# Rows on two queues, context turned later, and second projections in turns with a norm

## The reference

```python
def rms_norm(x, g):
    return x * lax.rsqrt(jnp.mean(x * x, axis=-1, keepdims=True) + EPS) * g
# first block, layer 0
hn = rms_norm(x, g_pre[0])
proj = hn @ ssm_w_in          # z, xBC and dt: dt is 32 columns wide
# between the blocks: the final norm of the first, and the first norm of the second
h = rms_norm(h, g_final)
hx = modulate(rms_norm_2(h, norm1), shift, scale)
# second block: keys, values, low-rank gate inputs (lr, 32 columns) of tokens and context
hx @ w_in; hc @ w_in[:, :CTX_COLS]
# MLP: squared ReLU, 1024 -> 4096 -> 1024
h = h + gate * (jnp.square(jax.nn.relu(modulate(rms_norm_2(h, norm2)) @ w_mlp1)) @ w_mlp2)
```

## Time and profile before

| | |
|---|---|
| median of three runs | 1840.89 us (1839.2 to 1844.04) |
| the profiled execution | 1845.2 us, its span 1843.4 us |
| PE busy | 1756.7 us, 95% |
| DVE busy | 1004.4 us, 54% |
| ACT busy | 798.3 us, 43% |
| POOL busy | 713.5 us, 39% |
| mean granted clock of PE | 0.981 |

### The profile page before, as it was taken

The page is one execution under the profiler, slowest core; times in us unless marked ns, Lnnn a source line. Parts: engine busy times, 40 slices in busy tenths (PEclk is TensorE's granted clock), DMA queues, the critical chain, the costliest instruction groups (busy, mean ns, idle before and its releaser), DMA issues.

```text
span 1843.4 us, 24950 instructions
## 1 busy us (share of the span) xinstructions
PE 1756.7 (95%) x8893; PEld 1401.0 (76%) x8893; DVE 1004.4 (54%) x1545; ACT 798.3 (43%) x1359; POOL 713.5 (39%) x795
## 2 busy tenths in 40 slices
PE   7999999988999889899999999999999989999998
PEld 5778777766776557678878788888878768888887
DVE  5788786677346773356649737656733341212122
ACT  4345463555456663345542235554432342323131
POOL 3644544434352105221113422223234645555553
PEclk9999999999999999999999999999999989999999
DMA  6342423121222002111028711121123323333332
GB/s 199 96 132 74 134 74 87 58 69 54 75 80 64 24 12 61 53 45 29 24 77 271 223 46 35 35 58 46 46 80 93 101 69 93 102 92 101 92 97 98
DMA packets 238794, 152.04 MB, mean 82 GB/s; under 512 B 7997, under 2 KB 223046, under 8 KB 238694
## 3 DMA queue, kind: packets, MB, share of 16 engines
q1 hardware_dynamic: 225894, 125.54, 23.6%
q10 hardware_dynamic: 12800, 25.17, 4.0%
HBM read 148.59 MB, written 2.10 MB: 82 GB/s over the span
## 4 chain that ended last, share of the span: by engine, by line
PE 65%; issue 12%; POOL 8%; DVE 8%; ACT 6%; DMA 1%; SPq 1%; POOLq 0%; DVEq 0%; ACTq 0%
PE ps L650 16%; PE ps L654 16%; PE ps L651 16%; POOL wl L600 8%; PE ps L2093 2%; PE ps L2075 1%; PE ps L1574 1%; PE ps L1606 1%; PE ps L2082 1%; PE ps L2555 1%; DMA ada_late<-w_ada 1%; DVE mod_late L2407 1%; DVE queries L1843 1%; PE ps L2076 1%; DVE pairs L2785 1%
## 5 line engine op out<-in xcount | busy, mean ns | idle before, releaser
L600 POOL TENSOR_TENSOR wl<-raw,wh 128x256 fp32r<-128x256 f32 (+1 forms) x775 | 690.1, 920 | 1070.1 <-ACT wh L613 1070.1
L650 PE MATMUL ps<-ah,wh 128*128 128x512 f32 (+1 forms) x1144 | 467.0, 408 | 16.5 <-DVE al L762 9.8
L654 PE MATMUL ps<-ah,wl 128*128 128x512 f32 (+1 forms) x1144 | 450.9, 394 | 0.1
L651 PE MATMUL ps<-al,wh 128*128 128x512 f32 (+1 forms) x1144 | 450.3, 394 | 0.0
L613 ACT ACTIVATE wh<-raw 128x1024 fp32r<-128x1024 f32 (+1 forms) x220 | 230.9, 1049 | 315.9 <-PE ps L654 302.7
L650 PEld LDWEIGHTS ps<-ah,wh 128*128 128x128 f32 (+1 forms) x1144 | 216.3, 189 | 78.2 <-issue 19.6
L654 PEld LDWEIGHTS ps<-ah,wl 128*128 128x128 f32 (+1 forms) x1144 | 216.1, 189 | 50.6 <-POOL wl L600 1.4
L651 PEld LDWEIGHTS ps<-al,wh 128*128 128x128 f32 (+1 forms) x1144 | 216.7, 189 | 45.0 <-issue 1.4
L650 PE MATMUL ps<-bh,wh 128*128 128x512 f32 (+1 forms) x588 | 233.7, 397 | 8.9 <-DVE bl L1427 3.3
L654 PE MATMUL ps<-bh,wl 128*128 128x512 f32 (+1 forms) x588 | 230.5, 392 | 0.9 <-POOL wl L600 0.8
L651 PE MATMUL ps<-bl,wh 128*128 128x512 f32 (+1 forms) x588 | 230.3, 392 | 0.0
(11 more groups left out here) (422 smaller groups left out, 2698.7 us busy)
## 6 DMA issues: line engine op xcount, KB each, us to landing
raw<-w_mlp SPq DMA_DIRECT2D x64, 512.0 KB, 3.8
raw<-w_in SPq DMA_DIRECT2D x52, 512.0 KB, 3.7
raw<-ssm_w_in SPq DMA_DIRECT2D x40, 512.0 KB, 3.8
ada_late<-w_ada ACTq DMA_DIRECT2D x16, 1024.0 KB, 6.8
ada_raw<-w_ada ACTq DMA_DIRECT2D x16, 512.0 KB, 3.7
raw<-ssm_w_out SPq DMA_DIRECT2D x16, 512.0 KB, 3.4
raw<-mla_w_in SPq DMA_DIRECT2D x11, 512.0 KB, 3.7
raw<-mla_w_out SPq DMA_DIRECT2D x8, 512.0 KB, 3.4
```

The lines of the kernel that those rows point to most:

```text
L600: nc.gpsimd.tensor_tensor(wl[:, s, part], raw[:, s, part], wh[:, s, part].bitcast(F32), ALU.subtract).then_inc(lo_ready, LOW_PIECES * (par ...
L650: nc.tensor.matmul(dst, w_hi[k], x_hi[k], start=k == 0, stop=False)
L651: nc.tensor.matmul(dst, w_hi[k], x_lo[k], start=False, stop=False)
L654: ins = nc.tensor.matmul(dst, w_lo[k], x_hi[k], start=False, stop=k == n - 1)
```

## The change

Four edits:

1. The 18 transfers of vector rows are divided: SP issues every other one (`row_sources[0::2]`), ACT the others at its very start.
2. Context's transposes move from ahead of "dt" to behind unit 1 of "ssm_first" (`turn_ctx`); ACT's four copies move behind its copy of unit 1, and DVE's wait for them moves to before the memset of `conv_in`.
3. In the second block the two norm sums come ahead of the context value tiles, "final" gets bank 4 for its own (with a wait before the second key unit, which writes that bank). `project_v` goes over chunks outside and tiles inside and waits for low pieces one by one. "lr" and the token tiles of value unit 0 run in turns, two chunks of "lr" and one of values.
4. The first MLP block is written out of the loop, and its units 0 and 1 run chunk by chunk in turns behind the norm.

```diff
+        def load_rows(eng, sources):
+            for name, col in sources:
+                v = as_rows(ins[name])
+                eng.dma_start(vrows[col % P:col % P + v.shape[0], col // P, :], v).then_inc(rows_in, 16)
...
@@ pe_start
-            pe.wait_ge(sem("ctx_in"), 16)
-            pe.wait_ge(sem("x_copied"), DC)
-            for c in range(DC):
-                for t in range(CTX // P):
-                    ins_ = nc.tensor.transpose(bank(CTX_BANKS[c // 2])[:, c % 2 * CTX + t * P:c % 2 * CTX + (t + 1) * P],
-                                               ctx_tok[:, t, c * P:(c + 1) * P], ident[:])
-                if c % 2:
-                    ins_.then_inc(sem("ctx_turned"), 1)
@@ pe_mamba
+            def turn_ctx():
...
             for n in range(1, 10):
                 projection("ssm_first", 0, n)
-                if n == 3:
+                if n == 1:
+                    turn_ctx()
+                elif n == 3:
                     turn_dt()
@@ act_start
             count_ahead(act, "act")
+            load_rows(act, row_sources[1::2])
             nc.scalar.preload_act_table_set(LN_EXP)
@@ act_mamba
-            take_ctx(0)
             split_ahead(act, "dt", 0, 0)
...
-            for c in range(2, DC, 2):
+            take_conv("ssm_first", 0, 0, 1)
+            for c in range(0, DC, 2):
                 take_ctx(c)
-            take_conv("ssm_first", 0, 0, 1)
@@ dve_start, dve_mamba
-            dve.wait_ge(sem("ctx_turned"), DC // 2)
...
+            dve.wait_ge(sem("ctx_turned"), DC // 2)
             st(nc.vector.memset(conv_in[:, :, 0:PAD], 0.0))
@@ act_between
-        GAINED_BANK = 7
+        GAINED_BANK, FINAL_BANK = 7, 4
...
-            norm_act(act, "final", None, D, dst=norm_sq[:, 1])
+            norm_act(act, "final", None, D, b=FINAL_BANK, dst=norm_sq[:, 1])
@@ pe_gqa
                     pe.wait_ge(acc_free[1], ACC0["gqa"][1] + 1)
+                else:
+                    pe.wait_ge(norm_rstd, 2 * NORM_AT["final"][0] + 1)
...
-            def project_v(half, tiles):
+            lows = {}
+
+            def project_v(half, tiles, ks=range(V_KS)):
 
                 s = slot("gqa", half)
-                unit_ready(pe, "gqa", 0, half)
+                if ks[0] == 0:
+                    lows[half] = unit_high(pe, "gqa", 0, half)
                 vh, vl = flat(wh, s, FULL, V_KS), flat(wl, s, FULL, V_KS)
-                for t in tiles:
...
+                for k in ks:
+                    lows[half](k, KVH * HD)
+                    for t in tiles:
...
-            project_v(0, range(TT, KT))
             norm_pe_summed(pe, "norm1", norm_v[:, 2], GAINED_BANK)
-            norm_pe_summed(pe, "final", norm_v[:, 1])
+            norm_pe_summed(pe, "final", norm_v[:, 1], FINAL_BANK)
+            project_v(0, range(TT, KT))
             pe.wait_ge(acc_free[0], ACC0["lr"][0] + 1)
-            project(bank(0, slice(0, 32)), "lr", 0, chunk(ah), chunk(al), DC, 32, before=norm_chunk(pe, "norm1")).then_inc(unit_done, 1)
-            pe.wait_ge(norm_rstd, 2 * NORM_AT["final"][0] + 1)
-            project_v(0, range(TT)).then_inc(unit_done, 1)
+            ready = norm_chunk(pe, "norm1")
+            for k in range(DC):
+                lr_done = project(bank(0, slice(0, 32)), "lr", 0, chunk(ah), chunk(al), DC, 32, before=ready, ks=[k])
+                if k == DC - 1:
+                    lr_done.then_inc(unit_done, 1)
+                if k % 2:
+                    v_done = project_v(0, range(TT), [k // 2])
+            v_done.then_inc(unit_done, 1)
             project_v(1, range(KT)).then_inc(unit_done, 1)
@@ pe_end
-                for n in range(2 * DC):
+                first = isinstance(i, int) and i == 0
+                if first:
+                    lows = [unit_high(pe, "mlp", 0, n) for n in range(2)]
+                    for n in range(2):
+                        pe.wait_ge(acc_free[n], ACC0["mlp"][n] + 1)
+                    ready = norm_chunk(pe, "norm2")
+                    for k in range(DC + 1):
+                        if k < DC:
+                            done_0 = project(bank(0), "mlp", 0, chunk(ah), chunk(al), DC, P, before=ready, ks=[k], low=lows[0])
+                            if k == DC - 1:
+                                done_0.then_inc(unit_done, 1)
+                        if k:
+                            done_1 = project(bank(1), "mlp", 1, chunk(ah), chunk(al), DC, P, ks=[k - 1], low=lows[1])
+                    done_1.then_inc(unit_done, 1)
+                for n in range(2 if first else 0, 2 * DC):
@@ mlp_blocks
-            with eng.Fori(0, UNITS["mlp"][2] - 1) as i:
+            block(0)
+            with eng.Fori(1, UNITS["mlp"][2] - 1) as i:
@@ block.sync
-            for name, col in row_sources:
-                v = as_rows(ins[name])
-                sp.dma_start(vrows[col % P:col % P + v.shape[0], col // P, :], v).then_inc(rows_in, 16)
+            load_rows(sp, row_sources[0::2])
```

More of the change, by code:

```diff
@@ L869, in projection @@
                 project(bank(n % 2), stage, n, chunk(ah), chunk(al), DC, P, low=low).then_inc(unit_done, 1)
+            def turn_ctx():
+                pe.wait_ge(sem("ctx_in"), 16)
+                pe.wait_ge(sem("x_copied"), DC)
+                for c in range(DC):
+                    for t in range(CTX // P):
+                        ins_ = nc.tensor.transpose(bank(CTX_BANKS[c // 2])[:, c % 2 * CTX + t * P:c % 2 * CTX + (t + 1) * P],
+                                                   ctx_tok[:, t, c * P:(c + 1) * P], ident[:])
+                    if c % 2:
+                        ins_.then_inc(sem("ctx_turned"), 1)
             def turn_dt():
@@ L2027, in sum_k @@
                 nc.tensor.matmul(bank(7)[:, 0:CTX], ones[:], k_sq[n][:, T:TA], start=True, stop=True).then_inc(sem("k_sums"), 1)
-            def project_v(half, tiles):
+            lows = {}
+            def project_v(half, tiles, ks=range(V_KS)):
                 s = slot("gqa", half)
-                unit_ready(pe, "gqa", 0, half)
+                if ks[0] == 0:
+                    lows[half] = unit_high(pe, "gqa", 0, half)
                 vh, vl = flat(wh, s, FULL, V_KS), flat(wl, s, FULL, V_KS)
-                for t in tiles:
[L2035 to L2039, removed]
+                for k in ks:
+                    lows[half](k, KVH * HD)
+                    for t in tiles:
+                        dst = bank((6, 7, 3)[t // 2])[:, t % 2 * CTX:(t % 2 + 1) * CTX]
+                        hi, lo, tok = (ah, al, t) if t < TT else (ch, cl, t - TT)
+                        tok, c = slice(tok * P, (tok + 1) * P), half * V_KS + k
                         nc.tensor.matmul(dst, hi[:, c, tok], vh[:, k], start=half == 0 and k == 0 and t % 2 == 0, stop=False)
@@ L2042, in project_v @@
                         ins_ = nc.tensor.matmul(dst, lo[:, c, tok], vh[:, k], start=False, stop=c == DC - 1 and t % 2 == 1)
-                    if half and t in (1, 3):
-                        ins_.then_inc(sem("gv_projected"), 1)
+                        if half and k == V_KS - 1 and t in (1, 3):
+                            ins_.then_inc(sem("gv_projected"), 1)
                 return ins_
-            lows = {}
             def project_q(j, ks):
                 if ks[0] == 0:
-                    lows[j] = unit_high(pe, "gqa", 0, q_unit(j))
+                    lows[KVH + j] = unit_high(pe, "gqa", 0, q_unit(j))
                     pe.wait_ge(acc_free[0], ACC0["gqa"][0] + 2 * j + 1)
-                ins_ = project(bank(0), "gqa", q_unit(j), chunk(ah), chunk(al), DC, P, ks=ks, low=lows[j])
+                ins_ = project(bank(0), "gqa", q_unit(j), chunk(ah), chunk(al), DC, P, ks=ks, low=lows[KVH + j])
                 if ks[-1] == DC - 1:
@@ L2097, in pe_gqa @@
             project_ctx("lr", 0, bank(1, slice(0, 32), slice(0, CTX)), 32).then_inc(sem("lr_ctx"), 1)
+            norm_pe_summed(pe, "norm1", norm_v[:, 2], GAINED_BANK)
+            norm_pe_summed(pe, "final", norm_v[:, 1], FINAL_BANK)
             project_v(0, range(TT, KT))
-            norm_pe_summed(pe, "norm1", norm_v[:, 2], GAINED_BANK)
-            norm_pe_summed(pe, "final", norm_v[:, 1])
             pe.wait_ge(acc_free[0], ACC0["lr"][0] + 1)
-            project(bank(0, slice(0, 32)), "lr", 0, chunk(ah), chunk(al), DC, 32, before=norm_chunk(pe, "norm1")).then_inc(unit_done, 1)
-            pe.wait_ge(norm_rstd, 2 * NORM_AT["final"][0] + 1)
-            project_v(0, range(TT)).then_inc(unit_done, 1)
+            ready = norm_chunk(pe, "norm1")
[6 more added lines that the diff above has]
+            v_done.then_inc(unit_done, 1)
             project_v(1, range(KT)).then_inc(unit_done, 1)
@@ L2920, in block @@
                     x = (ah, al) if n < DC else (bh, bl)
-                    ready = {0: norm_chunk(pe, "norm2"), DC: hidden}.get(n)
+                    ready = hidden if n == DC else None
```

(2 more changed lines are left out.)

## The result

| | before | after |
|---|---|---|
| median | 1847.17 us (20 executions, 1838.94 to 1851.26) | 1839.65 us (20 executions, 1833.58 to 1842.51) |
| the profiled execution | 1845.2 us, span 1843.4 | 1836.28 us, span 1834.5 |
| mean granted clock in it | 0.981 | 0.984 |

The ratio is 0.9969, with a 95% interval from 0.9954 to 0.9983: 5.7 us won (3.1 to 8.5), where 7.9 were forecast. The time itself, 1839.65, lies 6.65 above the forecast of 1833.0 and 0.15 outside its range. Nearly all of that gap is already in the first column: the forecast stood on 1840.89, the median of three executions, and twenty of the same kernel (these three among them) give 1847.17. The two medians lie 7.5 us apart and the two means 7.0, both inside the interval; that 7.5 comes near the forecast's 7.9 confirms nothing.

The account below looks back on a forecast made before the run. The prediction took TensorE (PE) as the bound, busy 1756.7 of 1843.4 us, so only its idle or slow-clock time could shrink. 0.6 + 5.7 + 1.6 = 7.9 us off 1840.9 gave 1833.0, range 1828.5 to 1839.5.

Parts of the forecast that it names:

- 0.6 us won was forecast: First stage: sum of 2.4 us won by an earlier dt and 1.8 lost to the moved transposes.
- the term of 2.4 (1.8 to 2.9): First stage: dt and unit 0 start earlier and end at 31.4 to 32.5 us instead of 34.3.
- doesn't start by 16: First stage: sign that the forecast is wrong; the norm was to start at 15.5 us.
- The second term: First stage: context's 16 transposes, moved behind the second unit into a full stretch, cost 1.8 us at full clock.
- 5.7 forecast: Second block: earlier norm sums and lr in turns with values end values at 770.9 us, against 776.6.
- 1.6 forecast: MLP: units 0 and 1 in turns win 2.4 us, less 0.85 idle at unit 2; ends -0.1 and 2.4.
- The stall ahead of unit 2: MLP: PE idles 0.5 us for unit 2's high half and 0.35 for its low half, 0.85 together.
- The late rise of the clock: Rival, first stage and MLP: clock rises late or falls again; 3.8 us won in all, 1837.1; chance 0.13.
- The moved transposes: Rival, first stage: they let the clock fall and unit 2 begins slow; 6.2 us won, 1834.7; chance 0.03.
- ACT was held: Rival, first stage: ACT's row issues make x's copies two microseconds late; 5.9 us won, 1835.0; chance 0.07.
- The second block's attention: Rival: attention takes the gain back, 5.7 falls to about 1; sum 3.2 us won, 1837.7; chance 0.09.
- The change of bank: Rival, second block: value matmuls changing bank half slow to 0.23 us apart; 7.9 us lost, 1848.8; chance 0.05.

Follow-up runs that it names:

- e10: After with context's transposes back in front, MLP unit 1 three chunks behind unit 0, and extra unread matmuls around the MLP's norm sum: 1833.16 us, ratio 0.9925 to before.
- e7: After plus extra matmuls, results unread, behind the vectors' transposes and around the last norm's sum: 1834.15 us, ratio 0.9964 to before.
- e4: Before with only the MLP edit (first block out of the loop, units 0 and 1 in turns): 1849.69 us, ratio 1.0008 to before.
- e3: Before with only the second block's edit: 1839.59 us, ratio 0.9957 to before.
- e1: Before with only the two first-stage edits (rows on two queues, context's transposes behind unit 1): 1848.82 us, ratio 0.9989 to before.
- e8: After with unit 1 of the first MLP block three chunks behind unit 0 instead of one: 1841.06 us, ratio 0.9975 to before.
- e2: Before with only the rows on two queues, context's transposes left in front: 1839.69 us, ratio 0.9956 to before.
- e5: After with context's transposes put back ahead of dt, the other edits kept: 1833.82 us, ratio 0.9956 to before.

## Why the prediction was right or wrong

**The base was the step that failed.** I subtracted 7.9 from 1840.89 and allowed "1.6 us either way for the spread of the runs", though the profiled execution, 4.3 us higher, lay before me. The 79 further executions of before that came with the experiments say how wide it is. Grouped by their mean granted clock (19 at 0.981, 0.982 and 0.984 lie between; one at 0.975 took 1851.8):

| mean granted clock | executions of before | mean time, us |
|---|---|---|
| 0.985 | 12 | 1839.1 |
| 0.983 | 9 | 1841.9 |
| 0.980 | 12 | 1845.7 |
| 0.977 to 0.979 | 18 | 1850.2 |
| 0.976 | 8 | 1851.1 |

That is 12 us from end to end, and on average 1.3 us for each 0.001 of clock, though not evenly. 0.001 of 1845 us is 3.7 us at half speed, so a slow microsecond costs some 0.36 us (an estimate from the table), less than the half that a full PE would lose; that part of it lies beside waits is the likely reason, not a measured one. The stretch from the group sums to lr shows nearly the same slope: 316.0 us with 10.2 us slow, 318.7 to 319.0 with 17.1, 324.2 with 34.1, that is 8.2 us for 24, 0.34 each. The code of the stretch is the same in all kernels up to e10. The three executions of the start lay at 1839 to 1844, in the quicker half of the twenty. With the profiled execution as the base the forecast would have been 1837.3, which is 2.4 from the median; by the mean of all 99 executions, 1845.2, it is 1837.3 as well, and after's mean is 1838.9.

**First stage: 0.6 us won was forecast, 1.0 lost in the pair of profiles.** The second step that failed is the term of 2.4 (1.8 to 2.9) for an earlier start of dt and unit 0. They were to be through at 31.4 to 32.5 instead of 34.3. Unit 1, which follows them, starts here, before and after:

```profile
34.59 0.47 PE L650 MATMUL ps<-ah,wh 128*128 128x512 f32 x1
```
```profile
33.85 0.47 PE L650 MATMUL ps<-ah,wh 128*128 128x512 f32 x1
```

So the term measured 0.7. Part of it is the norm, which started at 16.01 and not at 15.5 (`rstd` was done at 15.89), just beyond the sign "doesn't start by 16". The larger part is the clock. I had it slow from dt's start and counted its rise from there, to 22 or at the latest 24; it was still at 1.00 when dt started at 18.70, fell at 19.6 and rose at 26.4, and 13 matmuls stood 0.43 us apart instead of 7 to 11. With the clock held (e7) unit 1 starts at 31.60, 3.0 us ahead of before. The second term was right (1.7 measured at full clock, 1.8 forecast).

The size depends on the place of the fall. In e4, with before's code there, the clock fell as late as in after (0.75 in the slice from 19, so at 19.5):

```profile
20.37 3.68 PE L835 MATMUL ps<-ident,ctx_tok 128*128 128x128 f32 x16 [3.36 <-DMA ctx_tok<-ctx]
...
86.50 1.47 PE L888 MATMUL ps<-ident,xs 128*128 128x128 f32 x12
```

Against that, after is 0.5 us ahead. With before's code the stage ended at 84.98, 85.03 (e3) and 86.50, with both edits at 85.98, 85.11 (e1) and 85.25 (e8): 1.0 lost to 1.4 won by the pair, where my ends were 1.8 lost and 1.1 won, and no gain on average. What was never priced is the version that won: I wrote that before they "covered both a wait and the slow stretch", and then moved them without asking what they would cost if they stayed with the rows early. e2 shows it, 3.0 us, because context, moved forward by the same 3 us, is turned before the first `al`.

**Second block: 5.7 forecast, 5.5 measured** in after and in e3. Its steps held too: sums 3.5 earlier (3.7), first `al` written by 749.1 (748.95), a wait of 1.1 us for the second value unit (1.10), end at 770.9 (770.87), value matmuls 0.12 us apart. The measured times hold the 0.2 us that after was ahead at the start of the stretch.

**MLP: 1.6 forecast, 1.4 measured.** The clock was back 4.0 us after the start (1476.88 less 1472.90), 3.8 forecast. The stall ahead of unit 2 was taken as 0.85; it measured 0.9 in the starts of the matmuls, and taking it away with a lag gave 0.8 (e8).

**The rivals.** The late rise of the clock happened in the first stage and not in the MLP; it is what makes the first stage negative in after's profile. The moved transposes did not let the clock fall: they ran 1.91 us for 16 at the clock of 1.00 and the matmuls behind them stand 0.23 us apart. That is no test by itself, since PE's idle time of 2.02 us in e2 did not bring a fall either. What weighs more is e5, where the 16 transposes alone, from 17.01 to 20.39, stand ahead of the rise at 20.8, as before's do ahead of 23.5. There the traces do not agree with the rule of the Trainium skill, "TensorE: Matmul & The Clock Gate", Part 4: PE-mode transpose, that transposes do not count as PE being busy. ACT was held by 0.2 us only. The second block's attention took nothing back: from the queries' projection to the first scores it is 29.0 us in both (776.63 to 805.6, and 770.87 to 799.9). The change of bank costs the value matmuls nothing.

So the sum was 7.9, the stages give 7.4 where the clock falls alike (0.5 + 5.5 + 1.4) and 5.9 with the first stage as in the pair of profiles, and the ratio gives 5.7 (3.1 to 8.5), which fits either.

## What to carry to other kernels

Before a forecast in microseconds, look for how far executions of one kernel lie apart: where a clock falls in PE's gaps, three executions do not place a median, and a change of 5 us is read from the stages, each beside a stage of the same slow time. Work that filled a wait was free there at either clock; before such work is moved into a full stretch, price the version in which it stays and everything else of the change is done. Two remedies for one gap (here a lag and extra matmuls) need not add up.

## What was not expected of the hardware

- The clock's falls differ from profile to profile in unchanged code: the slow time between the group sums and lr was anything from 10.2 to 34.1 us in twelve profiles of the same instructions (before, after, e1 to e10), and the time of an execution followed its mean granted clock by 1.3 us for each 0.001. What decides the pattern of one execution, and whether the edits have a part in it, stays open.
- A fall is paid by its place. In front, context's 16 transposes took 1.97 or 3.38 us by the clock, and the stage ended at 82.02 and 81.95 alike; behind unit 1 the same stage ended at 83.75 without a fall, at 85.11 and 85.25 with one at 18.1 and 18.2, and at 85.98 with one at 19.6 (dt started at 18.33 to 18.70 in these).
- DVE's steps of a norm beside POOL's subtractions were slower by a half to three quarters. In after, while POOL splits from 16.91 to 21.42:

```profile
17.53 1.02 DVE L762 SCALAR_TENSOR_TENSOR al<-norm_v,ah 128x512 fp32r<-128x512 f32 x1
18.48 1.22 DVE L757 SCALAR_TENSOR_TENSOR norm_v<-resid,vec,rstd 128x512 f32<-128x512 f32 x1
19.62 1.21 DVE L762 SCALAR_TENSOR_TENSOR al<-norm_v,ah 128x512 fp32r<-128x512 f32 x1
```

Once POOL had ended, the same steps of the same norm took 0.68 (`al`, 21.89) and 0.74 (product, 22.49), and in the second block, with POOL idle, 0.75 (748.20). The second `al` was so written at 20.8, where 20.4 was forecast: an earlier norm met more of POOL's work. Which resource the two engines share was not tested.
